# A four-layer decoder trunk on one core: part of the convolution's taps moved from TensorE to DVE, and three reorderings

## The chip, the cores and the metric

The kernel runs on one core of a Trainium2 chip, as one launch. A core has TensorE (PE), VectorE (DVE), ScalarE (ACT), GpSimd (POOL) and SyncE (SP), each with its own queue of instructions that runs strictly in the order in which the kernel writes it, and each waiting for the others only through semaphores. The metric is the device time of a launch in microseconds; lower is better. Times given are medians of several executions, and one more execution is recorded by the hardware profiler.

## The reference

The program is one inference step for 512 prompt tokens and 64 sample tokens (8 sequences of 8) with a width of 1024, in float32. Four layers: gMLP, Conformer convolution, latent attention (MLA), gMLP. Each layer has a mixer and a SwiGLU FFN of width 2816, both with adaLN conditioning, a residual and a LayerNorm. The convolution module is what most of the change touches:

```python
def conv_module(h, ctx, w_pw1, b_pw1, w_dw, b_dw, ln_g, ln_b, w_pw2, b_pw2):
    a = h @ w_pw1 + b_pw1
    a = a[..., :D_MODEL] * jax.nn.sigmoid(a[..., D_MODEL:])
    full = jnp.concatenate([ctx, a], 1)
    y = lax.conv_general_dilated(full, w_dw[:, None, :], window_strides=(1,), padding='VALID',
                                 dimension_numbers=('NWC', 'WIO', 'NWC'),
                                 feature_group_count=D_MODEL) + b_dw      # 31 taps per channel
    y = jax.nn.silu(layer_norm(y, ln_g, ln_b))
    return y @ w_pw2 + b_pw2, full[:, -(CONV_WIDTH - 1):]
```

In the attention layer `d = h @ w_down` is cut into 384 query latents, 256 key latents and 64 rotary columns; the first two are RMS-normalised, the last rotated. The FFN is `(silu(h @ wg) * (h @ wu)) @ wd`.

## The kernel before

Activations are kept transposed, channels on partitions in 8 tiles of 128 and the 576 tokens along the free dimension, in two halves of 288. Weights come from HBM in units of 1024 columns through five slots (SP's queue); GpSimd splits each unit into an upper part (`w_hi`, L1001) and the rest (`w_lo`, L1004), and every product is made of three passes in a reduced-precision float32 form: upper by upper, rest of the activation by upper, upper by rest of the weight (L1153 records all matmuls). PSUM has 8 banks: 0 to 3 take the products in turn (`acc_ready`, `acc_free`), 4 to 7 the auxiliary results (`aux_ready`, `aux_free`).

**Convolution (layer 1).** The loop runs over the 8 channel tiles m. TensorE makes the four half products of tile m + 2 (none for m = 0, 6 and 7; each half of gate and value), then tile m's taps: `x4` holds the gated rows of 32 channels at four shifts on 128 partitions, `diag` the tap weights spread on diagonals (GpSimd, L1013), and 8 groups g of 4 matmuls each, one for each 32 channels, add four taps at a time in one PSUM bank. Then come two transposes for the new state rows (L1776, L1778). ScalarE makes the sigmoid of a gate half (L2339) and issues the four DMAs that fill `x4` for tile m + 2 (`spread`, L2442). DVE's `taps(m)` gates tile m + 2's halves (L3292), completes its sample rows (L3334, L3336), adds tile m - 1 and its square to the running sums `s_sum` and `s_sq` (L3364), reduces the products that GpSimd made for the sample tokens (L3343), adds the bias on the way out of PSUM (L3367) and copies the state rows (L3350). ScalarE squares the tile (L2460). Tile 7's taps are made in two halves, with LayerNorm statistics between them.

**FFN.** From the fourth column tile on, gate and up of a tile are made by seven products in place of eight (`paired`, in the order 1, 6, 5, 7, 2, 3, 4), from sums of weights and of activations: t1, t3 and t4 are sums of activation tiles, s4 a sum of weights (`form_last`, L3049). Product 2 takes the bank of product 1, which is freed by DVE's L3084; that one reads ScalarE's copy of product 1 (L2317), which stands on ScalarE's queue behind the upper part of s4 (L2314). t4's sum is finished by L3155, its parts by L2309 (ScalarE) and L3159 (DVE). On ScalarE, `apply` (L2127) makes the modulated input in two halves; between them it runs `early`, the first two gates of what follows.

**Attention (layer 2).** DVE copies the token-major down projection to `dtok`; scales the queries; scales and rotates the key latents of the first four token tiles; TensorE transposes the queries three times over (five transposes each, two auxiliary banks each), and DVE splits each into `ql_hi` and `ql_lo` (L2643, L2645). Then TensorE waits for the key latents, transposes them (L1868) into banks 0 to 3, waits until ScalarE has copied these, and makes the ten rotary query products.

## Time and profile before

| | |
|---|---|
| median of 3 executions | 3003.37 us (3003.17 to 3003.87) |
| the profiled execution | 3006.55 us, span 3004.8 us |
| TensorE busy | 2908.9 us, 97% of the span |
| DVE, ScalarE, GpSimd busy | 1643.8, 926.0, 1699.8 us |
| mean granted TensorE clock | 0.991 of full speed (2.4 GHz) |
| chain that ended last | 81% TensorE, 7% DVE, 3% ScalarE, 2% GpSimd |

The span begins with the first recorded instruction and ends with the last; the execution's own time is 1.75 us longer. The first column of a timeline row is the start in microseconds, the second the time taken; what stands in brackets is how long the engine was idle before it, and what released it.

### The profile page before, as it was taken

What the parts mean: (1) busy time and instruction counts of PE and PEld (TensorE: products, weight loads), DVE (VectorE), ACT (ScalarE), POOL (GpSimd) and SP (SyncE); (2) the same over time, 40 slices, a digit from 0 to 9 for tenths busy, and PEclk for the clock granted to TensorE, in tenths of its full rate; (3) what the DMA queues carried; (4) which work ended last, traced back from release to release, by engine and by line L of the source; (5) the groups of instructions that cost most, each with busy time, mean ns of one, the idle gap of its engine ahead of it and who ended that gap; (6) DMA issues with size and microseconds to landing.
All of it is one profiled execution on the core that took longest, in us unless ns stands there. A gap on an engine that the chain in (4) does not pass through costs nothing.

```text
span 3004.8 us, 53453 instructions
## 1 busy us (share of the span) xinstructions
PE 2908.9 (97%) x21220; PEld 2681.8 (89%) x21220; DVE 1643.8 (55%) x3121; ACT 926.0 (31%) x1813; POOL 1699.8 (57%) x1177
## 2 busy tenths in 40 slices
PE   5999999999999999999989999999999999999997
PEld 4789999999976799999976689999997999999997
DVE  3153684636563784636565548463663536856363
ACT  2220142414230352414233315241423301425141
POOL 2546546868655445857620044685764465468685
PEclk8999999999999999999999999999999999999999
DMA  6643434333344434444321334444422333222332
GB/s 229 249 112 92 124 116 162 99 113 112 100 121 134 170 116 160 151 136 148 97 64 44 95 124 136 148 146 141 140 79 85 96 91 103 67 82 85 88 96 74
DMA packets 450485, 354.84 MB, mean 118 GB/s; under 512 B 26120, under 2 KB 424832, under 8 KB 437933
## 3 DMA queue, kind: packets, MB, share of 16 engines
q1 hardware_dynamic: 435744, 324.79, 35.1%
q10 hardware_dynamic: 14493, 26.63, 3.0%
q8 instruction: 169, 2.77, 0.4%
q14 instruction: 79, 0.65, 0.1%
HBM read 337.86 MB, written 5.25 MB: 114 GB/s over the span
## 4 chain that ended last, share of the span: by engine, by line
PE 81%; DVE 7%; issue 3%; ACT 3%; POOL 2%; DVEq 1%; DMA 1%; POOLq 1%; ACTq 1%; SPq 1%
PE pb L1153 79%; POOL w_lo L1004 1%; DMA ada_first<-in_ada_w 1%; DVE part L2778 1%; ACT h_hi L2145 1%; POOLq L1003 1%; ACT hf L2145 1%; DVE pb L2797 1%; PE pb L1989 1%; DVE xa L2804 0%; DVE h_lo L2828 0%; DVE pr L3107 0%; PE pb L1266 0%; DVE part L2773 0%; ACTq L2442 0%
## 5 line engine op out<-in xcount | busy, mean ns | idle before, releaser
L1001 POOL TENSOR_SCALAR w_hi<-w_raw 128x1024 fp32r<-128x1024 f32 (+2 forms) x272 | 295.9, 1088 | 751.0 <-DMA w_raw<-in_gmlp_w_in 275.7
L1004 POOL TENSOR_TENSOR w_lo<-w_raw,w_hi 128x1024 fp32r<-128x1024 f32 (+2 forms) x272 | 653.1, 2401 | 45.0 <-issue 45.0
L1153 PE MATMUL pb<-a_hi,w_hi 128*128 128x288 f32 x2176 | 593.8, 297 | 2.1 <-DVEq L3392 1.9
L1153 PE MATMUL pb<-a_lo,w_hi 128*128 128x288 f32 x2176 | 588.4, 294 | 0.0
L1153 PE MATMUL pb<-h_hi,w_hi 128*128 128x288 f32 x2144 | 563.9, 299 | 18.0 <-DVE pr L3084 7.9
L1153 PE MATMUL pb<-h_lo,w_hi 128*128 128x288 f32 x2144 | 545.6, 296 | 0.0
L1046 POOL TENSOR_TENSOR w_lo<-w_raw,w_hi 128x512 fp32r<-128x512 f32 x288 | 382.3, 1349 | 180.0 <-DVE s_raw L3049 83.2
L1153 PEld LDWEIGHTS pb<-h_hi,w_hi 128*128 128x128 f32 x2144 | 392.8, 188 | 33.4 <-DVE pr L3084 10.9
L1153 PEld LDWEIGHTS pb<-a_hi,w_hi 128*128 128x128 f32 x2176 | 408.3, 188 | 8.8 <-POOL a_lo L1071 4.2
L1153 PEld LDWEIGHTS pb<-a_lo,w_hi 128*128 128x128 f32 x2176 | 408.6, 188 | 0.8
L1153 PEld LDWEIGHTS pb<-h_lo,w_hi 128*128 128x128 f32 x2144 | 389.5, 189 | 0.0
L1153 PE MATMUL pb<-h_hi,w_lo 128*128 128x288 f32 x2144 | 358.1, 296 | 0.0
L1153 PE MATMUL pb<-a_hi,w_lo 128*128 128x288 f32 x2176 | 352.1, 295 | 0.3
L1153 PEld LDWEIGHTS pb<-h_hi,w_lo 128*128 128x128 f32 x2144 | 310.1, 188 | 0.5
L1153 PEld LDWEIGHTS pb<-a_hi,w_lo 128*128 128x128 f32 x2176 | 309.7, 188 | 0.9 <-POOL w_lo L1004 0.9
L2763 DVE SCALAR_TENSOR_TENSOR xa<-pb,gate,xa 128x288 f32<-128x288 f32 (+1 forms) x288 | 137.7, 479 | 269.1 <-PE pb L1153 268.0
L1153 PE MATMUL pb<-t_lo,w_hi 128*128 128x288 f32 x864 | 236.8, 295 | 0.0
L1153 PE MATMUL pb<-t_hi,w_hi 128*128 128x288 f32 x864 | 236.1, 296 | 0.0
L1153 PEld LDWEIGHTS pb<-t_hi,w_hi 128*128 128x128 f32 x864 | 162.2, 188 | 0.4
L1153 PEld LDWEIGHTS pb<-t_lo,w_hi 128*128 128x128 f32 x864 | 162.4, 188 | 0.0
L1054 POOL TENSOR_TENSOR w_raw<-w_raw 128x512 f32<-128x512 f32 x72 | 93.2, 1294 | 108.9 <-DVE pb L3040 108.9
L2255 ACT ACTIVATE w_hi<-pb 128x512 fp32r<-128x512 f32 x144 | 78.3, 597 | 239.7 <-DVE pb L3043 143.3
(379 smaller groups left out, 4875.9 us busy)
## 6 DMA issues: line engine op xcount, KB each, us to landing
ada_w<-in_ada_w SPq DMA_DIRECT2D x80, 1024.0 KB, 7.7
w_raw<-in_ffn_w_gate SPq DMA_DIRECT2D x88, 512.0 KB, 3.8
w_raw<-in_ffn_w_up SPq DMA_DIRECT2D x88, 512.0 KB, 3.8
w_raw<-in_gmlp_w_in SPq DMA_DIRECT2D x64, 512.0 KB, 4.2
w_raw<-in_ffn_w_down SPq DMA_DIRECT2D x64, 512.0 KB, 4.3
w_raw<-in_gmlp_w_out SPq DMA_DIRECT2D x32, 512.0 KB, 4.7
w_raw<-in_ffn_w_down SPq DMA_DIRECT2D x32, 384.0 KB, 3.9
w_raw<-in_conv_w_pw SPq DMA_DIRECT2D x24, 512.0 KB, 3.9
```

Source lines behind the costliest of these rows:

```text
L1001: nc.gpsimd.tensor_scalar(w_hi[:, s, 0:w], w_raw[:, s, 0:w], 1.0, 1.0, ALU.mult, ALU.mult).then_inc(split_hi, 1)
L1003: pool.drain()
L1004: nc.gpsimd.tensor_tensor(w_lo[:, s, 0:w], w_raw[:, s, 0:w], w_hi[:, s, 0:w].bitcast(F32), ALU.subtract).then_inc(split_lo, 1)
L1046: nc.gpsimd.tensor_tensor(out, src, hi.bitcast(F32), ALU.subtract).then_inc(done, 1)
L1054: nc.gpsimd.tensor_tensor(w_raw[:, su, 0:HALF_UNIT], w_raw[:, sg_, 0:HALF_UNIT], w_raw[:, su, 0:HALF_UNIT], ALU.subtract)
L1153: return nc.tensor.matmul(out, lhsT, rhs, start=start, stop=stop)
L1989: last = nc.tensor.transpose(pb[:, n % BANKS, i * P:(i + 1) * P], rows, ident[:])
L2145: last = fn(dst, xa[:, m, h * HALF:h * HALF + w], ACT.Identity, scale=cs[:, t % RING_T, m, 0:1], bias=cb[:, t % RING_T, m, 0:1])
L2255: fn(w_hi[:, SLOTS - 1, e * HALF_UNIT:(e + 1) * HALF_UNIT], pb[:, sum_banks[l][e], :], ACT.Copy).then_inc(form_hi, 1)
L2763: last_ = v.scalar_tensor_tensor(out=y, in0=ps[:, 0:w], scalar=gp, in1=y, op0=ALU.mult, op1=ALU.add)
L2778: v.reduce_sum(part[:, 1, n, half_cols(h)], sq[:, m0:m1, half_cols(h)].rearrange("p m t -> p t m"), AX.X)
L2797: v.reciprocal(self.rstd, self.rstd)
```

## The change

In the convolution TensorE makes only the first 6, 5, 5, 5, 5, 6, 8 and 8 groups of taps of the eight tiles (`PE_TAPS`), and the diagonals are made for these only. DVE adds the other taps, 7 + 4 x 11 + 7 = 58 in all, in the PSUM bank, each by one scalar_tensor_tensor over 512 tokens. ScalarE completes the sample rows, adds the bias on the way out of PSUM, and copies the state rows; GpSimd adds to the running sums. In the attention layer the query split is shared by ScalarE (upper part) and DVE (rest), the query products come before the key transposes, the key latents are made between DVE's copies of the query products, and the keys go through the auxiliary banks. In the FFN `form_last` of the first pair comes before the last sum of t4, and t4's two parts come after the copy of product 1 (ScalarE) and the second sum (DVE). In `apply` an activation of one column with the function of the coming gates (Silu or Sigmoid) stands before `early`.

The diff, cut: semaphores, the wider `epsl` and most unchanged lines are left out, and 8 columns of the indent; hunks are headed by the line of before.

```diff
@@ 117 @@
 XW = SEQ + QT * (TG - 1)
+PE_TAPS = (6, 5, 5, 5, 5, 6, TG, TG)
@@ 1011 @@
         last = nc.gpsimd.tensor_tensor(
-            diag[:, m % 2, q], mask4[:].unsqueeze(1).to_broadcast([P, TG, QC]),
-            w4[:, q, m, :].unsqueeze(2).to_broadcast([P, TG, QC]), ALU.mult)
+            diag[:, m % 2, q, 0:PE_TAPS[m]], mask4[:].unsqueeze(1).to_broadcast([P, PE_TAPS[m], QC]),
+            w4[:, q, m, 0:PE_TAPS[m]].unsqueeze(2).to_broadcast([P, PE_TAPS[m], QC]), ALU.mult)
@@ 1033 @@
             diagonals(m + 1)
+        if m >= 2:
+            pool.wait_ge(ysq_ready, m - 1)
+            pool.drain()
+            nc.gpsimd.tensor_tensor(s_sum[:], s_sum[:], yc[:, m - 2, :], ALU.add)
+            nc.gpsimd.tensor_tensor(s_sq[:], s_sq[:], sqy[:, m % 2, :], ALU.add).then_inc(q_done, 1)
@@ 1764 @@
-        for g in range(TG):
+        for g in range(PE_TAPS[m]):
...
                 last = mm(out[QC * q:QC * (q + 1), 0:c1 - c0], diag[:, m % 2, q, g, :],
-                          x4[:, m % 2, q, QT * g + c0:QT * g + c1], g == 0, g == TG - 1)
+                          x4[:, m % 2, q, QT * g + c0:QT * g + c1], g == 0, g == PE_TAPS[m] - 1)
@@ 1797 @@
         pe.wait_ge(x4_full[m % 2], 16 * QT * (m // 2 + 1))
+        conv_banks[m] = (BANKS + X.n % BANKS, BANKS + (X.n + 1) % BANKS)
...
         if m < KT - 1:
-            new_rows(pb[:, aux_bank(), :], m).then_inc(aux_ready, 1)
+            new_rows(pb[:, aux_bank(), :], m).then_inc(rows_turned, 1)
@@ 1855 @@
     pe.wait_ge(ql_scaled, 1)
+    ql_at.append(X.n)
     for k in range(3):
-        transposes([(tt * P, dtok[:, tt, k * P:(k + 1) * P]) for tt in range(4)])
-        transposes([(0, dtok[:, 4, k * P:(k + 1) * P])])
-    pe.wait_ge(kv_ready, 1)
-    pe.wait_ge(acc_free, G.n + BANKS)
-    for k in range(3):
-        for tt in range(TT):
-            rows = (ckv[:, tt, k * P:(k + 1) * P] if k < 2
-                    else kr2[:, tt, :, :].rearrange("p a n -> p (a n)"))
-            out = pb[:, k, tt * P:(tt + 1) * P] if tt < 4 else pb[:, 3, k * P:(k + 1) * P]
-            last = nc.tensor.transpose(out, rows, ident[:])
-        last.then_inc(kt_ready, 1)
-    pe.wait_ge(kt_copied, 5)
+        for tts in (range(4), (4,)):
+            b = aux_bank()
+            for tt in tts:
+                last = nc.tensor.transpose(pb[:, b, tt % 4 * P:(tt % 4 + 1) * P],
+                                           dtok[:, tt, k * P:(k + 1) * P], ident[:])
+            last.then_inc(ql_turned, 1)
+            X.up()
...
                       (lambda k: ql_hi[:, k, token_tile(tt)], lambda k: ql_lo[:, k, token_tile(tt)]))
+    pe.wait_ge(kv_ready, 1)
+    pe.wait_ge(aux_free, X.n + BANKS)
+    keys_at.append(X.n)
+    banks = [BANKS + (X.n + i) % BANKS for i in range(BANKS)]
+    for k in range(3):
+        for tt in range(TT):
+            rows = (ckv[:, tt, k * P:(k + 1) * P] if k < 2
+                    else kr2[:, tt, :, :].rearrange("p a n -> p (a n)"))
+            out = pb[:, banks[k], tt * P:(tt + 1) * P] if tt < 4 else pb[:, banks[3], k * P:(k + 1) * P]
+            last = nc.tensor.transpose(out, rows, ident[:])
+        last.then_inc(kt_ready, 1)
+    X.up(BANKS)
@@ 1903 @@
             absorb(h - 1)
+        else:
+            pe.wait_ge(aux_free, X.n + BANKS)
@@ 2131 @@
             if h:
+                if t % 2:
+                    fn(epsl[:, 4:5], epsl[:, 0:1], ACT.Silu)
+                elif t // 2 % 3 == 1:
+                    fn(epsl[:, 4:5], epsl[:, 0:1], ACT.Sigmoid)
@@ 2304 @@
         first_upper(l, 5, g0)
-        act.wait_ge(t_sum, 4 * l + 4)
-        act.wait_ge(t_lo_dve, 3 * l + 3)
-        fn(t4_hi[:], t4_raw[:], ACT.Copy).then_inc(t_hi, 1)
         G.up(8)
-        residuals(t, 10, 12)
...
         fn(sg[:, 0, :], pb[:, G.n % BANKS, 0:HALF], ACT.Copy).then_inc(pair_kept, 1)
+        if m == PAIRED_FROM:
+            act.wait_ge(t_sum, 4 * l + 4)
+            act.wait_ge(t_lo_dve, 3 * l + 3)
+            fn(t4_hi[:], t4_raw[:], ACT.Copy).then_inc(t_hi, 1)
+            residuals(t, 10, 12)
@@ 2441 @@
+    def complete(m):
+        fs = full_s(full[:, m % 3, :])
+        if m > 2:
+            act.wait_ge(prod_ready, m - 2)
+        fn(fs[:, :, 0:CTX], one(stT, m).rearrange("p (b r) -> p b r", b=DEC_B), ACT.Copy)
+        fn(fs[:, :, CTX:], bt(snew[:, m % 3, :]), ACT.Copy)
+        act.drain().then_inc(full_ready, 1)
+    def output(m):
+        ys, bd = one(yc, m, slice(SEQ, TOK)), one1(par, m, C_DW)
+        act.wait_ge(taps_summed, m + 1)
+        fn(one(yc, m, slice(0, SEQ)), pb[:, conv_banks[m][0], :], ACT.Identity, bias=bd
+           ).then_inc(aux_free, 1)
+        fn(ys, ys, ACT.Identity, bias=bd)
+        act.drain().then_inc(yc_ready, 1)
+    def state_rows(m):
+        act.wait_ge(rows_turned, m + 1)
+        for dst, n, c0 in ((st_p, CTX, 0), (st_s, NS, P)):
+            last = fn(dst[:, m * P:(m + 1) * P], pb[0:n, conv_banks[m][1], c0:c0 + P], ACT.Copy)
+        last.then_inc(aux_free, 1)
@@ 2453 @@
             spread(m + 2)
-        act.wait_ge(yc_ready, m + 1)
+            complete(m + 2)
+        if m < KT - 1:
+            output(m)
+        else:
+            act.wait_ge(yc_ready, m + 1)
...
         fn(sqy[:, m % 2, cols], yc[:, m, cols], ACT.Square).then_inc(ysq_ready, 1)
+        if m < KT - 1:
+            state_rows(m)
@@ 2515 @@
     square_sums(1, KVR, QR, range(4))
+    def query_upper(k):
+        b_p, b_s = [BANKS + (ql_at[0] + 2 * k + i) % BANKS for i in range(2)]
+        act.wait_ge(ql_turned, 2 * k + 2)
+        fn(ql_hi[:, k, 0:SEQ], pb[:, b_p, :], ACT.Copy)
+        fn(ql_hi[:, k, SEQ:], pb[:, b_s, NS:P], ACT.Copy).then_inc(ql_upper, 1)
+    for k in range(2):
+        query_upper(k)
     square_sums(1, KVR, QR, range(4, TT))
-    for k in range(3):
-        act.wait_ge(kt_ready, k + 1)
-        fn(ckvT[:, k, 0:SEQ] if k < 2 else krT[:, 0:SEQ], pb[:, k, :], ACT.Copy).then_inc(kt_copied, 1)
-    fn(ckvT[:, :, SEQ:], pb[:, 3, 0:2 * P].rearrange("p (k t) -> p k t", k=2)[:, :, NS:], ACT.Copy
-       ).then_inc(kt_copied, 1)
-    fn(krT[:, SEQ:], pb[:, 3, 2 * P + NS:3 * P], ACT.Copy).then_inc(kt_copied, 1)
+    query_upper(2)
@@ 2530 @@
                   ).then_inc(kv_out, 16)
+    key_banks = [BANKS + (keys_at[0] + i) % BANKS for i in range(BANKS)]
+    for k in range(3):
+        act.wait_ge(kt_ready, k + 1)
+        fn(ckvT[:, k, 0:SEQ] if k < 2 else krT[:, 0:SEQ], pb[:, key_banks[k], :], ACT.Copy
+           ).then_inc(aux_free, 1)
+    ps = pb[:, key_banks[3], :]
+    fn(ckvT[:, :, SEQ:], ps[:, 0:2 * P].rearrange("p (k t) -> p k t", k=2)[:, :, NS:], ACT.Copy)
+    fn(krT[:, SEQ:], ps[:, 2 * P + NS:3 * P], ACT.Copy)
+    act.drain().then_inc(aux_free, 1)
@@ 3075 @@
     u23, u4, c11, c12, c22 = pr[:, 0, :], sg[:, 1, :], sg[:, 0, :], sg[:, 1, :], pr[:, 1, :]
-    form_last(l, m)
     if m != PAIRED_FROM:
+        form_last(l, m)
@@ 3085 @@
     v.tensor_tensor(u4, p5, u23, ALU.add)
+    if m == PAIRED_FROM:
+        dve.wait_ge(t_hi, 4 * l + 4)
+        v.tensor_tensor(t4_lo[:], t4_raw[:], t4_hi[:].bitcast(F32), ALU.subtract).then_inc(t_low, 1)
@@ 3151 @@
         first_product(5, g0, 1)
+        form_last(l, ms[0])
...
         first_lower(l, 5, g0, 1)
-        dve.wait_ge(t_hi, 4 * l + 4)
-        v.tensor_tensor(t4_lo[:], t4_raw[:], t4_hi[:].bitcast(F32), ALU.subtract).then_inc(t_low, 1)
@@ 3354 @@
         if m < KT - 2:
-            for h in range(2):
-                gated_in(m + 2, h, h)
+            gated_in(m + 2, 0, 0)
+            if m:
+                dve.wait_ge(full_ready, m)
+            gated_in(m + 2, 1, 1)
             dve.drain().then_inc(rows_ready, 1)
-            complete(m + 2)
-        if m:
-            dve.wait_ge(ysq_ready, m)
-            for acc, y in ((s_sum, yc[:, m - 1, :]), (s_sq, sqy[:, (m - 1) % 2, :])):
-                last_ = v.tensor_tensor(acc[:], acc[:], y, ALU.add)
-            last_.then_inc(q_done, 1)
-        sample_taps(m)
-        v.tensor_scalar(one(yc, m, slice(0, SEQ)), pb[:, aux(), :], one1(par, m, C_DW), None, ALU.add
-                        ).then_inc(aux_free, 1)
-        dve.drain().then_inc(yc_ready, 1)
-        state_rows(m, aux()).then_inc(aux_free, 1)
+        dve.wait_ge(prod_ready, m + 1)
+        v.reduce_sum(bt(one(yc, m, slice(SEQ, TOK))), prods[m % 2][:], AX.X).then_inc(prod_used, 1)
+        sums_ = pb[:, aux(), :]
+        for w in range(QT * PE_TAPS[m], CW):
+            v.scalar_tensor_tensor(out=sums_, in0=full[:, m % 3, w:w + SEQ], scalar=wdT[:, m, w:w + 1],
+                                   in1=sums_, op0=ALU.mult, op1=ALU.add)
+            dve.drain()
+        dve.drain().then_inc(taps_summed, 1)
+        X.up()
...
     m, bd = KT - 1, one1(par, KT - 1, C_DW)
+    dve.wait_ge(yc_ready, KT - 1)
@@ 3455 @@
-    def latents(n, t0, t1):
+    def scale_keys(n, t0, t1):
@@ 3464 @@
                                    scalar=ssq[:, tt, 1:2], in1=gqk[:, QR:], op0=ALU.mult, op1=ALU.mult)
+    def turn_keys(t0, t1):
@@ 3481 @@
-    def evac_latents(ks):
-        for k in ks:
-            for cols, src in ((slice(0, SEQ), slice(0, SEQ)), (slice(SEQ, TOK), slice(NS, P))):
-                split(ql_hi[:, k, cols], ql_lo[:, k, cols], pb[:, aux(), src]).then_inc(aux_free, 1)
+    def query_lower(k):
+        dve.wait_ge(ql_upper, k + 1)
+        for cols, src in ((slice(0, SEQ), slice(0, SEQ)), (slice(SEQ, TOK), slice(NS, P))):
+            v.tensor_tensor(ql_lo[:, k, cols], pb[:, aux_of(X.n), src], ql_hi[:, k, cols].bitcast(F32),
+                            ALU.subtract).then_inc(aux_free, 1)
+            X.up()
+    def query_rows(n):
+        c, tt = divmod(n, TT)
+        dve.wait_ge(acc_ready, G.n + 1)
+        v.tensor_copy(qrt[:, tt, c * 256:(c + 1) * 256], pb[:, G.n % BANKS, 0:256]).then_inc(acc_free, 1)
+        G.up()
@@ 3499 @@
                 scale_queries()
-            if tt == TT - 2:
-                latents(2, 0, 4)
-    evac_latents((0,))
-    latents(3, 4, TT)
+    for k in range(3):
+        query_lower(k)
+    dve.drain().then_inc(lat_ready, 1)
+    scale_keys(2, 0, 4)
+    for n in range(2):
+        query_rows(n)
+    turn_keys(0, 4)
+    for n in range(2, 5):
+        query_rows(n)
+    scale_keys(3, 4, TT)
+    turn_keys(4, TT)
     dve.sem_inc(kv_ready, 1)
-    evac_latents((1, 2))
-    dve.drain().then_inc(lat_ready, 1)
-    for c in range(2):
-        for tt in range(TT):
-            dve.wait_ge(acc_ready, G.n + 1)
-            v.tensor_copy(qrt[:, tt, c * 256:(c + 1) * 256], pb[:, G.n % BANKS, 0:256]
-                          ).then_inc(acc_free, 1)
-            G.up()
+    for n in range(5, 10):
+        query_rows(n)
+    X.up(BANKS)
```

## Rows read from the trace of the kernel before

**Rows 1.** The page, part 1: busy time, share of the span, instructions.

```profile
PE 2908.9 (97%) x21220; PEld 2681.8 (89%) x21220; DVE 1643.8 (55%) x3121; ACT 926.0 (31%) x1813; POOL 1699.8 (57%) x1177
```

**Rows 2.** Two tiles: length, each engine's busy time, clock, DMA share, GB/s.

```profile
893.20:913.20 20.00, 20.00 (x163) 14.81 (x162) 13.76 (x15) 1.58 (x3) 15.97 (x10) 1.00 0.45 109
933.20:953.30 20.10, 20.10 (x165) 14.91 (x164) 6.77 (x12) 1.69 (x3) 13.36 (x9) 1.00 0.43 108
```

**Rows 3.** TensorE's timeline: tile 0's taps and what follows them.

```profile
864.30 7.08 PE L1153 MATMUL pb<-x,diag 128*32 128x512 f32 x64
...
873.13 0.40 PE L1153 MATMUL pb<-h_hi,w_hi 128*128 128x288 f32 x1 [1.43 <-DVE full L3292]
```

**Rows 4.** Instructions by source line: count, ns min/median/max, first and last start.

```profile
L3043 DVE TENSOR_TENSOR pb<-pb,w_raw x72: 698/700/700, 451.6 to 2918.7; 128x512 f32<-128x512 f32 x72
...
L2763 DVE SCALAR_TENSOR_TENSOR xa<-pb,gate,xa x288: 439/472/521, 245.3 to 2988.5; 128x288 f32<-128x288 f32 x124, 128x224 f32<-128x224 f32 x20
...
L3343 DVE TENSOR_REDUCE yc<-prod x8: 2205/2210/2221, 877.3 to 989.2; 128x64 f32<-128x1984 f32 x8
...
L3364 DVE TENSOR_TENSOR s_sum<-s_sum,yc x6: 757/759/4580, 890.9 to 977.0; 128x576 f32<-128x576 f32 x6
...
L1004 POOL TENSOR_TENSOR w_lo<-w_raw,w_hi x272: 994/2400/3482, 9.5 to 2958.5; 128x1024 fp32r<-128x1024 f32 x114, 128x768 fp32r<-128x768 f32 x18, 128x384 fp32r<-128x384 f32 x4
```

**Rows 5.** ScalarE's timeline: the residuals, and one tile's four DMA issues.

```profile
863.63 8.41 ACT L2162 ACTIVATE xa<-xa,ab,ag 128x288 f32<-128x288 f32 x16 [14.71 <-issue]
...
913.47 4.33 ACTq L2442 DMA_DIRECT2D x<-full  x4
```

**Rows 6.** Tile 7's taps in TensorE's timeline; x4's DMAs from 973 to 985.

```profile
984.39 0.94 PE L1153 MATMUL pb<-x,diag 128*32 128x288 f32 x12 [0.72 <-issue]
...
x<-full ACTq DMA_DIRECT2D x4, 270.0 KB, 7.9
```

**Rows 7.** The first pairs in FFN 0 and 1: timelines, and one stretch.

```profile
465.80 0.40 PE L1153 MATMUL pb<-h_hi,w_hi 128*128 128x288 f32 x1 [0.67 <-DVE pr L3084]
...
477.70 0.40 PE L1153 MATMUL pb<-h_hi,w_hi 128*128 128x288 f32 x1 [0.52 <-DVE pr L3084]
...
1125.15 2.51 DVE L3155 TENSOR_TENSOR t_raw<-t_raw,h_lo 128x1152 f32<-128x1152 f32 x1 [0.20 <-issue]
...
1130.38 0.69 DVE L3049 TENSOR_TENSOR s_raw<-w_raw,pb 128x512 f32<-128x512 f32 x1
...
1132.64 0.40 PE L1153 MATMUL pb<-h_hi,w_hi 128*128 128x288 f32 x1 [1.82 <-DVE pr L3084]
...
1132.60:1136.40 3.80, 3.75 (x17) 3.76 (x18) 3.27 (x7) 2.17 (x4) 2.33 (x2) 0.56 0.02 4
```

**Rows 8.** Timelines: a table load in layer 3, TensorE's waits behind the gates.

```profile
834.72 0.54 PE L1153 MATMUL pb<-h_hi,w_hi 128*128 128x288 f32 x2 [0.70 <-DVEq L2837]
...
2594.98 1.28 ACT L2203 ACT_TABLE_LOAD   x1 [5.33 <-PE pb L1153]
...
2599.17 0.54 PE L1153 MATMUL pb<-h_hi,w_hi 128*128 128x288 f32 x2 [2.69 <-DVEq L2837]
```

**Rows 9.** The attention layer's transposes: DVE, TensorE, and two stretches.

```profile
1545.12 0.69 DVE L2643 CAST ql_hi<-pb 128x512 fp32r<-128x512 f32 x1
1545.89 0.69 DVE L2645 TENSOR_TENSOR ql_lo<-pb,ql_hi 128x512 fp32r<-128x512 f32 x1
...
1546.64 1.33 PE L1266 MATMUL pb<-ident,dtok 128*128 128x128 f32 x5 [5.38 <-DVE ql_lo L2645]
1549.40 0.90 PE L1868 MATMUL pb<-ident,ckv 128*128 128x128 f32 x3 [1.44 <-DVEq L3482]
...
1553.83 0.39 PE L1153 MATMUL pb<-w_hi,ql_hi 128*128 128x256 f32 x1 [0.97 <-ACT krT L2524]
...
1546.60:1554.00 7.40, 4.95 (x21) 4.16 (x22) 5.35 (x19) 2.08 (x5) 1.55 (x3) 0.58 0.91 264
1554.00:1565.00 11.00, 11.00 (x93) 11.00 (x93) 3.89 (x10) 0.00 (x0) 4.48 (x6) 1.00 0.29 83
```

More of the change, by code:

```diff
@@ L206, in trunk @@
         mtmp = sb("mtmp", [P, KT, NC])
-        epsl = at("epsl", [P, 2], F32, top[0] - 32)
+        epsl = at("epsl", [P, 8], F32, top[0] - 32)
         ada_row_at = region(size([P, TOK]))
@@ L433, in trunk @@
         taps_done = sem("taps_done")
+        taps_summed = sem("taps_summed")
+        rows_turned = sem("rows_turned")
         last_tile = sem("last_tile")
@@ L447, in trunk @@
         kt_ready = sem("kt_ready")
-        kt_copied = sem("kt_copied")
+        ql_turned = sem("ql_turned")
+        ql_upper = sem("ql_upper")
         ql_scaled = sem("ql_scaled")
@@ L757, in trunk @@
         turn_at = []
+        conv_banks = {}
+        ql_at, keys_at = [], []
         stat_banks = {}
```

## The prediction, made before the changed kernel was built or run

> **What bounds the kernel now.** I read the first part of the page, then the stretches between two convolution tiles, then TensorE's idle times in order of time, and behind each the instruction that ended it. TensorE is busy for 2908.9 of 3004.8 us [rows 1]: a gain is either matmul work taken off it, or one of its waits, or a stretch that it ran at the low clock after a wait. In the convolution it is busy all of the time, 20.05 us a tile (mean of 20.00 and 20.10), while DVE is busy for 6.8 to 13.8 us and GpSimd for 13.4 to 16.0 [rows 2]. The sum is made against the profiled execution's 3006.55 us (1.75 us around the span); the median shown, 3003.37, is 3.2 us less.
>
> **Convolution, matmuls removed.** A tile of 8 tap groups takes 7.07 us [rows 3], with the last matmul's own tail in it, so a group is 0.87 us. Tiles 1 to 4 lose 3 groups each, 12 x 0.87 = 10.4 us; tiles 0 and 5 lose 2 each, 1.7 us. The saving counts only where nothing else ends TensorE's next wait.
> - Tile 0: behind it TensorE already waits 1.43 us for DVE's gated rows [rows 3]. These wait for ScalarE's gate, which starts when 16 residual instructions end (863.63 + 8.41 = 872.04) [rows 5]; none of this depends on the taps. Its 1.7 us become wait: 3.1 us idle in one piece. 1.82 us of idle in layer 1 were followed by a stretch of 3.8 us at a mean granted clock of 0.56 [rows 7], part of it at 1.2 GHz in place of 2.4, which costs 0.44 x 3.8 = 1.6 us; the 1.43 us here were not. I count 0 gained and 1.6 lost; bounds 0 and -1.7.
> - Tiles 1 to 4: 10.4, if DVE, ScalarE and GpSimd keep up with 20.05 - 2.6 = 17.4 us (below).
> - Tile 5: 1.7, but tile 7's taps, two tiles on, waited 0.72 us for something the trace names no releaser for, and its x4 copies take 7.9 us to land behind 4 MB of adaLN weights [rows 6]. I take 1.0, between 0 and 1.7.
>
> **Does DVE keep up?** Added: 58 scalar_tensor_tensor of 128x512, read from SBUF and PSUM, written to PSUM, each with a drain. This form isn't in the trace. From below: tensor_tensor with the same two homes and size, 0.70 us; from above: scalar_tensor_tensor of 128x288, at most 0.52, by columns 0.93 [rows 4]. Start to start over a drain two dependent instructions are 0.77 us apart, 0.08 more than one lasts [rows 9]. I take 0.78 + 0.08 = 0.86 (bounds 0.78 and 1.01): 11 taps 9.5 us, 58 taps 50. Three gated rows (at most 1.5) and the sample reduction (2.2) [rows 4] make 13.2 us a tile. DVE becomes the bound at (17.4 - 3.7)/11 = 1.25 us a tap, and the tile is slower than before at 1.49. The Trainium skill (VectorE: DVE Perf Modes, The DRAIN you can't avoid) states a flush of about the duration less 266 ns behind every DVE instruction; an estimate by that page is 0.78 + 0.51 = 1.29 us a tap, and DVE would be the bound by 0.04 x 11 = 0.4 us a tile; the 0.77 us pair speaks against it.
>
> More is at stake in blocking. GpSimd works for most of the tile, and a DVE addition of two SBUF tiles that takes 0.76 us took 4.58 once; the additions with one input in PSUM never exceeded 0.70 in 72 cases [rows 4], GpSimd or not. The taps are of the second kind. What leaves DVE (two running sums, copies, bias) was partly of the first.
>
> ScalarE per tile: two gates, 4.3 us of DMA issues [rows 5], now also two copies, bias of 512 and 64 columns, the square, two state-row copies: some 4 us by the 0.5 to 0.7 us that such instructions take. In order: taps summed at 9.5 after the matmuls' end, bias, square and rows until 11.7, and only then the next tile's first gate, queued behind the wait for the sums, until 12.3, DVE's gated row 12.8. TensorE asks for that bank at 17.4: slack 4.6. The last gate's pair is ready at 13, DVE ends its reduction at 16.8, before the next tile's sums: slack 0.6, and lateness there is not passed on at once, as the output bank is needed only two tiles later.
>
> GpSimd per tile: 13.36 busy [rows 2] (its diagonals get shorter, which I leave out), plus two sums of 576 columns (w_lo's 1024 take 2.40 [rows 4], by columns 1.35, I take 1.45): 16.3 of 17.4. In the tail the sums and the products wait for ScalarE's copies, so the five weight splits behind them start about 5 us later and run into DVE's a_lo subtractions, which are of the blocked kind: 0.3 lost.
>
> **Tables.** The gate's ACT_TABLE_LOAD stood behind TensorE's product (5.33 us of ScalarE idle, 1.28 of load, then the gates) [rows 8]. Now a dummy draws it into that idle time; the half-block that follows on ScalarE and DVE starts 1.28 earlier. TensorE waits there for 2.69 us in layer 3 and 0.70 before the convolution [rows 8]; in layers 0 to 2 it has adaLN matmuls to run and no such wait. Gain 1.28 + 0.70 = 2.0. The Trainium skill (ScalarE: Activation LUTs, What ACT_TABLE_LOAD costs) puts a switch at 2.66 us with its drain; by that the gain would be 2.66 + 0.70 = 3.4, but the rows show the gates start 1.29 us behind the load's start.
>
> **FFN.** PSUM bank 0 is freed by DVE's L3084, which waits for ScalarE's copy, which stands behind the copy of s_raw, which waits for L3049, which stands behind t4_lo and the t4 sum, L3155. In layer 1: L3155 at 1125.15 for 2.51, L3049 at 1130.38, TensorE released at 1132.64 after 1.82 us [rows 7]. With form_last ahead of L3155, s_raw is made at some 1125.8 and copied while L3155 runs; L3084 then follows L3155 (1127.66) and one subtraction of 0.5, near 1128.3, while TensorE is through its fourth product at 1130.8 (1132.64 - 1.82). The wait goes (four layers: 0.67, 1.82, 1.86, 1.81; two shown). So does the low clock behind the last three, 1.6 each. What is late next: t4_lo (1.36) now lies between L3087 and the sums of the second pair, and GpSimd's s_lo can block it; layer 0 shows the second pair's wait, 0.52 [rows 7], which layers 1 to 3 hid by the low clock. I take 0.8 in each. Layer 0: 0.67 - 0.3 = 0.4. Layers 1 to 3: 3 x (1.83 + 1.6 - 0.8) = 7.9. Sum 8.3, bounds 2 (the second wait brings the low clock back) and 10.
>
> **Attention.** TensorE waits 5.38 + 1.44 + 0.97 = 7.8 us around the two sets of transposes, and the clock is 0.58 over 7.4 us with 4.95 busy: 0.42 x 4.95 = 2.1 lost [rows 9]. The first wait is for the first query split, which DVE begins at 1545.12, behind the key latents in its queue. Afterwards DVE and ScalarE share the split at once: ScalarE's copies of 512 and 64 columns 0.8 us, DVE's two subtractions 0.9. The third pair of transposes waits about 0.9, the products about 1.95 for the last split: 2.85, and I expect one low-clock stretch behind it, 1.6. The key latents then run under the ten query products, which fill the 11.0 us from 1554 on [rows 9]: some 9 us of DVE work by its instructions of 0.2 to 0.5, ready about 2 us before TensorE asks. Gain 9.9 - 4.45 = 5.4, bounds 3 and 7. SP's loads behind d_ready (value weights, masks, head units) move ahead with it, GpSimd's splits too; four output DMAs on ScalarE's queue stand ahead of the key copies, 2.7 us, covered by the first head's two products.
>
> **Sum.** 10.4 + 0 - 1.6 + 1.0 - 0.3 + 2.0 + 8.3 + 5.4 = 25.2 us. 3006.55 - 25.2 = 2981.4 as profiled, 2978.2 as timed. A change below 0.2%, 6 us, can't be told from none.
>
> **Rivals.**
> - GpSimd or the ring DVE, ScalarE, DVE sets the tile. It decides once GpSimd's 16.3 or DVE's 16.8 us exceed 17.4, say by port conflicts. At the full 20.05 the 10.4 are lost: 2988.6. For: the slack is 1.1 and 0.6. Against: both lag by up to a tile without harm. Chance 0.10.
> - On the other side: the taps are blocked by GpSimd after all, as s_sum once was [rows 4]. The trace has no scalar_tensor_tensor with in0 in SBUF and in1 in PSUM. At 2.4 us a tap a tile takes 3.7 + 26.4 = 30 us: +10 in four tiles, +40 - (25.2 - 11.4) = +26: 3029. It decides at 1.49 us a tap for the tiles, and at about 1.8 for the whole. The Trainium skill (SBUF — State Buffer, Who interferes with whom) says that an instruction with at most one SBUF input does not contend; the 72 rows agree. Chance 0.04.
> - The low clock does not come back (tile 0, attention): 3.2 more, 2975; with small second waits in the FFN, 2973. For: 1.43 us of idle did not bring it [rows 3]. Against: 1.82 did [rows 7]. Chance 0.2.
> - The waits move rather than go: attention 3, FFN 2 to 4: 2985. Chance 0.13.
> - The forecast, 2974 to 2983: chance 0.53.
>
> From 2971 to 2988 some 8 in 10 are held: below lies a part of the clock's case, above it the blocked taps and most of the first rival. Faster 0.94 (all but the blocked taps and 2 in 100 in which several gains fail), same 0.02, slower 0.04.
>
> **What would show it.** Right: tile windows of 17.4 us with TensorE full from tile 1 to 4; 58 instructions of 0.7 to 0.9 us, longest near the median; no L3084 wait in the first pair, one below 1 us in the second; two waits near 0.9 and 2 us before the queries and none before the keys; a wait of 3 us behind tile 0. Wrong: taps with a long tail of durations; TensorE waiting for w_lo or the gated rows in tiles 2 to 5; a low clock in tiles 1 to 4; the keys awaited.

## The result and the profile after

The changed kernel takes 2978.2 us (median of 4 executions, 2974.5 to 2981.6) against 3003.6 (4 executions, 3003.2 to 3004.7): a ratio of 0.9915 with a 95% interval of 0.9897 to 0.9932. The forecast was 2978.2, range 2971 to 2988. The profiled execution is the shortest of the four, 2974.5 us with a span of 2972.4. It gained 32.4 us of span, seven more than the 25.4 between the medians; where the seven come from is told below.

The first part of the page, which answers to [rows 1]:

```profile
span 2972.4 us, 53309 instructions
PE 2887.9 (97%) x21092; PEld 2669.5 (90%) x21092; DVE 1643.3 (55%) x3121; ACT 941.8 (32%) x1864; POOL 1713.7 (58%) x1189
```

TensorE's busy time fell by 21.0 us and the rest of the span by 11.4. Two tiles, by windows (columns: window, its length, busy time of PE, PEld, DVE, ACT, POOL, granted clock, DMA share, GB/s), and the new instruction by its line:

```profile
889.40:906.80 17.40, 17.40 (x142) 14.03 (x138) 11.62 (x16) 3.59 (x9) 16.91 (x12) 1.00 0.51 124
924.20:941.60 17.40, 17.40 (x142) 14.07 (x138) 11.62 (x16) 3.63 (x9) 16.39 (x12) 1.00 0.51 128
```

```profile
L3440 DVE SCALAR_TENSOR_TENSOR pb<-full,wdT,pb x58: 745/755/758, 874.6 to 966.6; 128x512 f32<-128x512 f32 x58
```

Against [rows 2] a tile is 2.65 us shorter and TensorE is as full as before. All 58 taps take 745 to 758 ns; nine in a row take 7.39 us, so 0.83 from one to the next. GpSimd is busy for 16.4 and 16.9 of the 17.4 us, where 16.3 had been forecast.

TensorE's idle times by the timeline (start of the instruction that ended the wait, its duration, then in brackets the wait and its releaser), those that answer to [rows 3], [rows 6], [rows 7], [rows 8] and [rows 9]:

```profile
477.53 0.40 PE L1164 MATMUL pb<-h_hi,w_hi 128*128 128x288 f32 x1 [1.06 <-DVE pr L3156]
...
871.88 0.40 PE L1164 MATMUL pb<-h_hi,w_hi 128*128 128x288 f32 x1 [2.84 <-DVE full L3366]
973.76 1.61 PE L1164 MATMUL pb<-x,diag 128*32 128x288 f32 x21 [1.83 <-issue]
...
1128.21 0.40 PE L1164 MATMUL pb<-h_hi,w_hi 128*128 128x288 f32 x1 [0.78 <-DVE pr L3156]
...
1523.44 0.77 PE L1875 MATMUL pb<-ident,dtok 128*128 128x128 f32 x5 [0.99 <-DVE ql_lo L3565]
1525.91 0.58 PE L1164 MATMUL pb<-w_hi,ql_hi 128*128 128x256 f32 x1 [1.71 <-DVEq L3591]
1534.50 0.39 PE L1164 MATMUL pb<-w_hi,ql_hi 128*128 128x256 f32 x1 [0.60 <-DVE qrt L3573]
1538.83 0.39 PE L1164 MATMUL pb<-w_hi,ql_hi 128*128 128x256 f32 x1 [0.84 <-DVE qrt L3573]
...
2570.39 0.53 PE L1164 MATMUL pb<-h_hi,w_hi 128*128 128x288 f32 x2 [2.18 <-DVEq L2909]
```

L3156 is the L3084 of before. Behind the 2.84 us comes a stretch at half clock, in windows:

```profile
873.40:876.80 3.40, 3.40 (x17) 3.40 (x16) 3.24 (x4) 0.02 (x1) 3.40 (x2) 0.50 0.85 125
877.00:889.40 12.40, 12.40 (x103) 10.14 (x105) 5.74 (x9) 3.37 (x9) 12.07 (x10) 1.00 0.44 131
```

TensorE is full in it at 0.50 (1.2 GHz), so it costs 1.7 us.

**Where the time went, step by step.** Each kernel was traced a second time (`before_again` and `repeat` below). The span is cut at the same TensorE instructions in all four traces; a gain is the stretch's length before less that after. The first pair is the first trace of each kernel, the second pair the second.

| stretch | predicted | first pair | second pair |
|---|---|---|---|
| FFN, layer 0 | 0.4 | 0.5 | 0.4 |
| to the first taps (gate table) | 0.7 | 0.7 | 1.0 |
| tile 0 | -1.6 | -1.2 | -2.9 |
| tiles 1 to 4 | 10.4 | 10.3 | 10.3 |
| tile 5 until tile 7's taps | 1.0 | 0.6 | 0.5 |
| convolution's tail | -0.3 | 0.1 | 0.1 |
| FFN, layers 1, 2, 3 | 7.9 | 3.7, 3.2, 2.6 | 3.8, 3.1, 1.8 |
| attention, until the first head's end | 5.4 | 4.3 | 4.1 |
| layer 3's wait (gate table) | 1.3 | 0.5 | 0.5 |
| **steps of the prediction** | **25.2** | **25.2** | **22.7** |
| not edited: start of layer 1 | 0 | 3.8 | 0.6 |
| not edited: all the rest | 0 | 3.4 | -3.2 |
| **span** | | **32.4** (3004.8 to 2972.4) | **20.1** (2999.2 to 2979.1) |

The steps account for what changed in their own stretches. The seven microseconds by which the first pair exceeds them are in stretches where nothing was edited. The last row also holds the products right behind layer 3's wait: the half clock there was in the kernel before in the first pair and in the changed kernel in the second, 1.0 us for and 1.0 against the change.

### The profile page after: what moved, and what is told of

It reads as the page before. It is cut to its first block, busy times and chain, and to the rows that moved or that the text cites. A ratio compares the mean times of both kernels' runs of the same rounds, so it can differ in the third digit from the quotient of the medians.

```text
span 2972.4 us, 53309 instructions
## 1 busy us (share of the span) xinstructions
PE 2887.9 (97%) x21092; PEld 2669.5 (90%) x21092; DVE 1643.3 (55%) x3121; ACT 941.8 (32%) x1864; POOL 1713.7 (58%) x1189
## 4 chain that ended last, share of the span: by engine, by line
PE 80%; DVE 8%; issue 3%; ACT 2%; POOL 2%; DVEq 1%; POOLq 1%; DMA 1%; ACTq 1%; SPq 1%
PE pb L1164 79%; POOL w_lo L1010 1%; DMA ada_first<-in_ada_w 1%; DVE part L2850 1%; POOLq L1009 1%; ACT h_hi L2171 1%; ACT hf L2171 1%; DVE pb L2869 1%; DVE xa L2876 1%; PE pb L2011 0%; DVE pr L3182 0%; DVE h_lo L2900 0%; DVE part L2845 0%; POOL w_lo L1057 0%; DVEq L2875 0%
```

## The experiments

**The changed kernel once more** (no edit).

> The changed kernel once more, nothing edited. Its first profiled execution gained 32.4 us of span (3004.8 to 2972.4) where the steps sum to 25.2, and its four times spread over 7 us (2974.5 to 2981.6), against 1.6 us for the kernel before. Theory A, phase: at the start of layer 1 DVE's L2788 and L2793 (all operands in SBUF) run beside or ahead of GpSimd's weight split by luck; in the kernel before they took 1.11 and 2.35 us, TensorE waited 2.62 us, and a 3.4 us stretch at half clock followed; here 0.23 and 0.93, no wait, full clock. In this second trace one or more of the three stretches that were at the low clock before (1050, 1730, 2600 us) comes back, each worth 1.3 to 3.8 us, and the span is 2974 to 2981. Theory B: these gains belong to the change; then the same two low-clock stretches (at the convolution's first tile and in the attention) and no other are seen, and the span is within 1 us of 2972.4. Ratio to before in both: 0.9905 to 0.993.

2979.5 us (5 executions, 2976.2 to 2983.8), ratio 0.9918 (0.9904 to 0.9931); profiled 2981.2, span 2979.1. Between 60 and 2950 us TensorE's records show 17.1 us at half clock, where the first trace had 6.8: at 64, 872 (twice as long), 1531 and 2576 us. Half of the difference is 5.1 us of time; 2.8 us more are waits (39.7 against 36.9 us of TensorE's idle time from 380 us on). The two overlap, since a wait costs nothing more at half clock; together they cover the 6.7 us between the two spans, and the clock has the larger part. Theory A holds in that stretches come back; but of the three that I had named only the one at 2600 did (at 2576), and DVE was ahead of GpSimd again.

**The kernel before once more** (no edit).

> The kernel before once more, nothing edited: a second trace of it. Its profiled execution took 3006.6 us, with 27.3 us of half clock between 60 and 2950 us and a wait of 2.62 us at 1050 us behind DVE's L2716 and L2721 at 1.11 and 2.35 us, which began 0.03 us after GpSimd's weight split. Theory: whether these two are blocked is decided by which engine starts first, and in most traces (seven of nine so far) DVE does; then they take 0.23 and 0.23 to 0.93 here, the 2.62 us wait is gone and the span is 2998 to 3003. Rival: in this kernel GpSimd always comes first, and the change moved that; then 1.11, 2.35 and 2.6 us again. The ratio to the kernel before is 1 within 0.001, which shows what the measurement can tell.

Median 3004.9 (10 executions, 3001.0 to 3007.8), ratio 1.0005 (0.9996 to 1.0014), so a difference of 0.1%, 3 us, can just be told. The trace has span 2999.2 and 13.7 us at half clock, against 27.3 in the first. At the start of layer 1, DVE and GpSimd by the timeline, first in the first trace of before, then in this one:

```profile
1033.30 1.11 DVE L2716 SCALAR_TENSOR_TENSOR cs<-mtmp,par 128x72 f32<-128x72 f32 x1
1034.33 0.22 DVE L2718 SCALAR_TENSOR_TENSOR mtmp<-mtmp,par 128x72 f32<-128x72 f32 x1
1034.62 2.35 DVE L2721 TENSOR_TENSOR cb<-cb,mtmp 128x72 f32<-128x72 f32 x1
...
1033.27 1.06 POOL L1001 TENSOR_SCALAR w_hi<-w_raw 128x1024 fp32r<-128x1024 f32 x1 [34.71 <-DMA w_raw<-in_conv_w_pw]
```

```profile
1033.69 0.23 DVE L2716 SCALAR_TENSOR_TENSOR cs<-mtmp,par 128x72 f32<-128x72 f32 x1
1033.84 1.08 DVE L2718 SCALAR_TENSOR_TENSOR mtmp<-mtmp,par 128x72 f32<-128x72 f32 x1
1034.99 0.23 DVE L2721 TENSOR_TENSOR cb<-cb,mtmp 128x72 f32<-128x72 f32 x1
...
1033.70 1.15 POOL L1001 TENSOR_SCALAR w_hi<-w_raw 128x1024 fp32r<-128x1024 f32 x1 [34.76 <-DMA w_raw<-in_conv_w_pw]
```

GpSimd starts 0.03 us ahead of L2716 in the one and 0.01 behind it in the other. From the start of L2716 to the end of L2721 DVE needs 3.67 us or 1.53; in the second trace L2718 is the one that is slow. The 2.1 us go down DVE's queue to the statistics, for which TensorE waits 2.62 us, or 0.23. With the half clock behind the longer wait that is the 3.8 us of the table: not the change's.

**The coefficients' rows in PSUM** (the edit, cut; L2788 and L2793 are the L2716 and L2721 of before).

```
-  add(mtmp[:], 0)                               # SBUF
+  mt = pb[:, bk, :].rearrange("p (b n) -> p b n", b=16)[:, 0:KT, 16:16 + NC]
+  add(mt, 0)                                    # a free part of the bank it reads
...
-  v.scalar_tensor_tensor(out=cs[:, tr], in0=mtmp[:], ...)
+  v.scalar_tensor_tensor(out=cs[:, tr], in0=mt, ...)
```

> The changed kernel with mtmp, the scale and shift rows from which DVE makes the adaLN coefficients, in a free part of the PSUM bank that they come from and not in SBUF: three instructions for each of seven sets have one SBUF input where they had two. Theory: DVE instructions with two SBUF inputs are the ones that GpSimd blocks. Then the first and the last of the three at the start of layer 1 take 0.22 to 0.3 us whatever GpSimd does beside them (0.23 and 0.93 in the changed kernel, 1.11 and 2.35 in the kernel before and in u23_apart), TensorE has no wait for the statistics at 1040 us in any run, and the times scatter less upward: 0.5 to 2 us faster in the median. Rival: GpSimd blocks them all the same, by the output in SBUF; then 0.9 to 2.4 us are seen again, and the time is the same within 1 us.

```profile
1026.28 0.23 DVE L2788 SCALAR_TENSOR_TENSOR cs<-pb,par 128x72 f32<-128x72 f32 x1
1026.73 0.23 DVE L2793 TENSOR_TENSOR cb<-cb,pb 128x72 f32<-128x72 f32 x1
...
1026.05 1.06 POOL L1007 TENSOR_SCALAR w_hi<-w_raw 128x1024 fp32r<-128x1024 f32 x1 [31.55 <-DMA w_raw<-in_conv_w_pw]
```

Here GpSimd started 0.23 us ahead of L2788, and nothing is blocked. In the seven traces of changed kernels in which L2793 ran under GpSimd's split with both inputs in SBUF, but L2788 had started first, it took 0.91 to 0.94. The time did not follow: 2979.6 us, ratio 0.9923 (0.9910 to 0.9937), the same as `repeat`, where 0.5 to 2 us had been expected. The event was rare in the changed kernels (one of ten traces with mtmp in SBUF, `u23_apart`), so there was little to win in the median.

**The taps' sum in SBUF** (the edit, cut: ScalarE's bias reads `yc` too).

```
-  v.scalar_tensor_tensor(out=sums_, in0=full[...], ..., in1=sums_)   # sums_ in PSUM
+  v.scalar_tensor_tensor(out=yc[:, m, 0:SEQ], in0=full[...], ..., in1=sums_)
+  sums_ = yc[:, m, 0:SEQ]
```

> DVE's taps keep their count and size, but their running sum is in SBUF: the first tap of a tile reads TensorE's bank and writes yc, the others (52 of 58) read full and yc and write yc, and ScalarE adds the bias there. In the changed kernel's traces all 58 taps took 746 to 758 ns with GpSimd busy for nearly all of the tile. The prediction's step: an addition with one input in PSUM isn't blocked by GpSimd, one with two inputs in SBUF is (0.76 us took 4.58 once). Then these 52 have a long tail or a median well above 0.76, the tiles 1 to 4 go from 17.4 to 22 to 30 us, TensorE waits there for the gated rows, and the kernel is 15 to 60 us slower. Rival: the home of the inputs doesn't matter, these additions just were short; then the taps stay at 0.75 to 0.8 us and the time within 2 us of the changed kernel. In between: only those taps that begin under an instruction of GpSimd wait for it, once each; at 10 or so such waits of 1 to 2.4 us a tile DVE needs 11 x 0.83 + 3.7 + 10 to 20.

```profile
L3440 DVE SCALAR_TENSOR_TENSOR yc<-full,wdT,yc x52: 750/791/4555, 877.4 to 995.7; 128x512 f32<-128x512 f32 x52
L3440 DVE SCALAR_TENSOR_TENSOR yc<-full,wdT,pb x6: 736/739/749, 876.6 to 985.0; 128x512 f32<-128x512 f32 x6
```

The 52 taps with two SBUF inputs take 79.2 us in all, 1.52 on average and up to 4.56; the six that read PSUM keep to 0.75. TensorE waits 2.3, 7.9 and 3.8 us for the gated rows of the tiles behind them, 4.2 more for ScalarE's bias ahead of tile 7's taps, and the time is 3002.7 us, ratio 0.9993 (0.9983 to 1.0002): the whole gain of the change is gone. GpSimd suffers too: its w_hi splits of 1.05 us had a median of 1.49. This is the rival "blocked by GpSimd", at a mean of 1.52 us a tap, and it shows that the input's home decided it: the six write SBUF just as the 52 do, and five of them ran beside a busy GpSimd. The Trainium skill (SBUF — State Buffer, Who interferes with whom) says that a DVE instruction with two SBUF inputs contends with a GpSimd instruction that reads SBUF, and that one with at most one SBUF input, outside the 2-port perf modes, does not; these rows agree.

**All taps on TensorE.**

```
-PE_TAPS = (6, 5, 5, 5, 5, 6, TG, TG)
+PE_TAPS = (TG,) * 8
```

> All 8 tap groups of every tile on TensorE, DVE adds no tap; ScalarE's bias, squares and copies and GpSimd's running sums stay as changed. By the prediction's sum the tiles 1 to 4 cost 10.4 more, tile 5 between 0.6 and 1.7, and tile 0 gives back the 1.6 of the low clock behind a longer wait: 9 to 11 us slower than the changed kernel, some 2988, with tiles of 20.0 us. If instead the shift of work to ScalarE and GpSimd were what gained in the tiles, the time would be within 3 us of the changed kernel. If the taps on DVE cost something elsewhere (late residual adds, blocked splits), the loss is below 8.

2988.8 us, ratio 0.9949 (0.9935 to 0.9963), 9.3 more than `repeat`, as expected. The removed matmuls are the gain of the convolution, and the move of the other work gains nothing by itself. Tile 0 is followed by a wait of 1.37 us and no half clock, as before the change.

**Tile 0 alone back on TensorE.**

```
-PE_TAPS = (6, 5, 5, 5, 5, 6, TG, TG)
+PE_TAPS = (TG, 5, 5, 5, 5, 6, TG, TG)
```

> Only tile 0 goes back to 8 groups on TensorE (its 7 taps leave DVE). Theory: tile 0 saved nothing, since the gated row came when it came, and the 2.84 us of idle behind it brought a 3.4 us stretch at half clock. With 8 groups the idle is 1.1 to 1.4 us, the clock stays full, tile 1's taps start some 1.5 us earlier relative to the wait's end, and the kernel is 1.0 to 1.8 us faster than the changed one. Rival: the low clock comes whatever the idle's length, then the time is the same within 0.5 us; or the two groups really were on the path, then it is 1.7 us slower.

2981.6 us, ratio 0.9925 (0.9912 to 0.9939), against 2979.5 for `repeat`: the 1.0 to 1.8 us expected did not come. Locally the theory held: 0.56 us of wait for the gated row, full clock, and from the last wait ahead of the convolution (817 us) to tile 1's taps it takes 67.9 us against 69.2 and 70.7 in the two traces of the changed kernel. But then two stretches of half clock stood at 974 and 1011 us, behind waits of 2.58 and 1.87 us. In the two traces of the changed kernel these waits are 1.83 and 1.95, 1.87 and 1.88 us, at the full clock. In this trace what tile 0 won was lost at them; that the edit brings the half clock there is not shown, since `coefs_psum` and `u23_apart`, with tile 0 as changed, have the second one too.

**Four groups on TensorE in tiles 1 to 4.**

```
-PE_TAPS = (6, 5, 5, 5, 5, 6, TG, TG)
+PE_TAPS = (6, 4, 4, 4, 4, 6, TG, TG)
```

> Tiles 1 to 4 keep 4 tap groups on TensorE instead of 5, DVE adds 15 taps in each instead of 11. In the changed kernel's trace nine taps take 7.39 us, 0.83 from one to the next, and DVE is busy for 11.6 of a tile of 17.4 us. Theory: a tile is then 17.4 - 0.87 = 16.53 us, DVE needs 15 x 0.83 + 3.7 = 16.15 and GpSimd some 16.3, so TensorE still sets it: 4 x 0.87 = 3.5 us faster than the changed kernel. Rival: the ring of sums, ScalarE's bias and gate, and DVE's gated row is what TensorE waits for; then the tile stays near 17.4 with TensorE idle in it, and the time is within 1 us. Rival: GpSimd at its limit slows the tiles, with waits for the weights' low parts, 0 to 2 us slower.

2981.3 us, ratio 0.9930 (0.9916 to 0.9944): not the 3.5 us faster that was expected. The rival of the ring holds. DVE and ScalarE in tiles 2 to 3:

```profile
923.88 0.52 DVE L3366 SCALAR_TENSOR_TENSOR full<-pb,par,sg 128x288 f32<-128x288 f32 x1 [2.90 <-ACT sg L2366]
...
927.21 12.38 DVE L3440 SCALAR_TENSOR_TENSOR pb<-full,wdT,pb 128x512 f32<-128x512 f32 x15
942.50 0.52 DVE L3366 SCALAR_TENSOR_TENSOR full<-pb,par,sg 128x288 f32<-128x288 f32 x1 [2.90 <-ACT sg L2366]
...
939.70 0.69 ACT L2484 ACTIVATE yc<-pb,par 128x512 f32<-128x512 f32 x1 [9.67 <-DVEq L3443]
941.88 0.87 ACT L2366 ACTIVATE sg<-pb,par 128x288 f32<-128x288 f32 x2
```

One turn is 942.50 - 923.88 = 18.6 us: 3.3 for gated rows and reduction, 12.4 for the taps, and 2.9 in which DVE stands idle while ScalarE adds the bias, squares, copies and only then makes the gate. TensorE could do a tile in 16.5 and waits, 1.02 and 1.74 us. The same idle time is in the changed kernel, with 11 taps:

```profile
920.34 0.52 DVE L3366 SCALAR_TENSOR_TENSOR full<-pb,par,sg 128x288 f32<-128x288 f32 x1 [2.91 <-ACT sg L2366]
```

There DVE waits 1.20 and 0.77 us more in a turn, for TensorE by way of the second gate and for the sums, so that TensorE sets the tile.

**The FFN's order put back** (last sums behind L3155, t4's split on ScalarE ahead of the first pair; the other edits stay).

```
-                    form_last(l, ms[0])
...
-                if m == PAIRED_FROM:
-                    dve.wait_ge(t_hi, 4 * l + 4)
-                    v.tensor_tensor(t4_lo[:], ...)
```

> Only the FFN's order is put back (last sums behind the product's sum, the fourth operand's split ahead of the first pair); the rest is as changed. Theory by the steps: layer 0 loses 0.4, layers 1 to 3 lose 1.8 of wait and 1.6 of low clock each and get 0.77 back: 3 x 2.64 + 0.4 = 8.3 us slower than the changed kernel, with waits for L3156 of 0.7 in layer 0 and 1.8 in each of the others and a 3.4 us stretch at half clock behind each of these three. Rival: the low clock depends on the phase of each run and not on the 1.8 us wait; then fewer than three such stretches are seen and the loss is 3.5 to 7 us.

2989.5 us, ratio 0.9950 (0.9936 to 0.9963), 9.9 more than `repeat`. By the traces' stretches it is 7.1: 0.9, 1.8, 2.6 and 1.8 for layers 0 to 3. The waits of 1.84, 1.82 and 1.84 us are back, but half clock stands behind the one in layer 2 only; where it is missing, the second pair's wait shows (0.53 in layers 1 and 3). The rival about the clock (fewer than three such stretches) was right; the 7.1 by the stretches is just above its 3.5 to 7, and the timed 9.9 is above both forecasts.

**The gate's table not drawn ahead** (the two dummy activations left out).

> Only the two dummy activations that draw the gate's table ahead are left out. By the prediction's step the kernel is 2.0 us slower than the changed one: 1.28 in layer 3, where TensorE waits for the second half's statistics (2.18 us in the changed kernel, 2.69 in the one before), and 0.70 at the convolution's entry, whose wait comes back. The traces gave 0.62 at the entry and 0.54 in layer 3, 1.2 together. Rival: TensorE's wait in layer 3 hangs on DVE, not on ScalarE's table; then it stays near 2.2 and only the convolution's 0.6 is lost.

2980.9 us, ratio 0.9930 (0.9915 to 0.9944): 3.6 us slower than `repeat` by the ratios, whose intervals overlap. The trace gives the size, 1.2 us where the prediction had 2.0: the wait at the convolution's entry is back at 0.69 us, and layer 3's is 2.69 where all others with the dummies have 2.17 to 2.31.

**The attention's order put back** (its edits in the diff above, reversed).

> Only the attention's order is put back (keys' transposes ahead of the queries' products, DVE alone splits the queries); the rest is as changed. By the prediction the kernel is 5.4 us slower than the changed one; its trace gave 4.3 between the last product before the transposes and the first head. The waits of 5.4, 1.4 and 1.0 us come back, and a stretch of 6.8 us at half clock. Rival: the low clock is luck here too (the changed kernel once more had 3.4 us of it in the attention, two other variants 6.8), then the loss is 2.5 to 3.5.

2983.9 us, ratio 0.9935 (0.9921 to 0.9949), 5.1 us slower than `repeat` by the ratios, whose intervals overlap a little. The waits are back at 5.39, 1.14 and 0.97 us, with 13.7 us of half clock. From the last products before the transposes to the first head's end it takes 84.5 us, against 78.9 in the changed kernel, some 5.5 more. The kernel before needs 1.2 to 1.4 less than this for the same stretch, with 6.8 us of half clock: that much of the loss is the clock's, and the rest agrees with the 4.3 and 4.1 of the table.

**A buffer of its own for the second pair's sum** (the edit, cut). In the changed kernel DVE idles for GpSimd before L3156:

```profile
1127.70 0.46 DVE L3156 TENSOR_TENSOR pr<-pb,sg 128x288 f32<-128x288 f32 x1 [3.04 <-POOL a_lo L1082]
...
1126.04 1.56 POOL L1082 TENSOR_TENSOR a_lo<-pr,a_hi 128x288 fp32r<-128x288 f32 x2
```

It waits only because the sum goes into the half of pr that GpSimd still reads.

```
+  spare = at("spare", [P, HALF], F32, a_at + HB // 2 + (KT - 1) * TOK * 4)
...
+  second = m == PAIRED_FROM + 1
+  if second: u23 = spare[:]
...
+  if second: dve.wait_ge(a_ready, 8 + a_before(l) + 2 * m)   # here, ahead of c22
```

> The changed kernel with one buffer more: in the FFN's second pair DVE writes the sum of L3156 into the idle last tile of a_lo and not over the gated values that GpSimd still reads (L1082), and waits for GpSimd only ahead of the write that follows later. Theory: the 0.77 to 1.06 us that TensorE waits for L3156 in each of the four layers are this wait, so they go: 3.4 us faster than the changed kernel, no wait for L3156 in any layer, and none for a later instruction of this pair. Rival: the wait moves to DVE's next additions (bank of the fourth product), still 0.5 to 1 us a layer, and nothing is gained. Rival: DVE's sum comes only after the copy of the first product by ScalarE, and half of it is gained.

2971.5 us, ratio 0.9893 (0.9878 to 0.9909), the lowest median of all, though its interval overlaps that of `repeat` a little. No wait for this instruction is left in any layer, and by the stretches of the four FFNs the gain is 0.9 to 1.1 each, 4.0 in all, against 3.4 expected. The rest of the 8 us between the medians stays unexplained: the trace is of the slowest of the four executions (2976.0), and the other three have none. This trace even caught the blocked coefficients:

```profile
1023.85 1.11 DVE L2789 SCALAR_TENSOR_TENSOR cs<-mtmp,par 128x72 f32<-128x72 f32 x1
1025.17 2.35 DVE L2794 TENSOR_TENSOR cb<-cb,mtmp 128x72 f32<-128x72 f32 x1
...
1023.83 1.05 POOL L1008 TENSOR_SCALAR w_hi<-w_raw 128x1024 fp32r<-128x1024 f32 x1 [31.76 <-DMA w_raw<-in_conv_w_pw]
...
1041.15 0.75 PE L1165 MATMUL pb<-part,ones 128*128 128x288 f32 x2 [2.59 <-DVEq L2852]
```

**Three edits together** (`u23_apart`, `coefs_psum`, and DVE's third query copy moved between the halves of the keys' rotation).

> The two edits together (the pair's sum in a buffer of its own, the coefficients' rows in PSUM), and in the attention DVE copies the third query product between the two halves of the keys' rotation. Expected against the changed kernel: 4.2 us from the first (four waits for L3156, as the trace of u23_apart gave them), 0.5 to 2 from the second, 0.3 to 0.8 from the third (of the waits of 0.6 and 0.84 us for the query copies one goes, but the keys are then ready about 0.8 us after TensorE asks for them): 5 to 7 us faster than the changed kernel, ratio to the kernel before 0.989 to 0.990. If the three took from one another (a wait that moves), it is 3 to 4.

2975.0 us, ratio 0.9908 (0.9893 to 0.9923), its span 2971.1: 4.5 us below `repeat` by the medians and 3.0 by the ratios, less than the 5 to 7 expected. The first edit's waits are gone again. Of the third the expected trade is seen: one query wait of 0.49 in place of 0.60 and 0.84, and a new wait of 0.64 for the keys. Its interval overlaps that of `u23_apart`; the two edits added have no gain that these runs show.

## Why the prediction was right, point by point

- **Tiles 1 to 4, 10.4:** 10.3 in both pairs. DVE's 0.86 us a tap was 0.83, and its work in a tile 12.4 (3.3 for rows and reduction, 9.1 for 11 taps) against 13.2. The estimate from the Trainium skill's flush (VectorE: DVE Perf Modes, The DRAIN you can't avoid), 1.29 us, is refuted for this case: the 0.77 us pair [rows 9] was the right row. "Taps with one input in PSUM are not blocked" is shown from both sides, by 745 to 758 ns in PSUM and by 750 to 4555 in SBUF.
- **DVE's bound was mis-sized,** though the forecast did not hang on it. I put it at (17.4 - 3.7)/11 = 1.25 us a tap, as if DVE worked through. `four_groups` shows that 2.9 us of every turn are idle, since the gated row waits for the sums by way of ScalarE: (17.4 - 3.3 - 2.9)/11 = 1.02. At five groups the turn is 15.3 us, 2.1 below the tile; at four it is 18.6 against 16.5. The 15.3 is reckoned from these parts, the 18.6 measured. I had called ScalarE's slack 4.6 and DVE's 0.6 and treated them as two; it is one ring. GpSimd's slack was smaller than said as well: 0.5 to 1.0 us a tile for 1.1.
- **Tile 0, nothing gained and 1.6 lost:** wait 2.84 and 3.34, clock at half, -1.2 and -2.9. The wait and the half clock came as said, but undoing it did not help (`tile0_8`).
- **Tile 5 and tail:** 0.6 for 1.0; the later splits of GpSimd cost nothing that shows.
- **Tables, 2.0:** 0.7 to 1.0 at the entry for 0.7, 0.5 in place of 1.28 in layer 3; this term was sized too high, and the larger 3.4 that stood beside it still more. The load's 1.28 us do come off the start of the gates, but then both gates and DVE's products wait for TensorE's last banks (0.60 to 0.73 us), which finish in that very stretch; the next bound was close behind.
- **FFN, 8.3:** 9.9 and 9.2. The second waits were as taken, 0.76 to 0.80, and the L3084 waits of the first pair are gone. What I had not counted is that the waits of 0.81 and 0.41 us for the same line in later pairs (1359 and 2128 us) went as well. The term for the clock was too sure: of nine waits of 1.81 to 1.86 us (first trace of before, `before_again`, `ffn_undone`), six had half clock behind them. In the second pair one of the three in the kernel before was missing (layer 3: 1.8 for 2.6), which hides part of what I had not counted.
- **Attention, 5.4:** 4.3 and 4.1. The two waits ahead of the products were 0.99 and 1.71, forecast 0.9 and 1.95, and one stretch of 3.4 us at half clock came. Missed: two waits of 0.60 and 0.84 us for the query copies. I had placed the key latents "under the ten query products" by their sum of work; but the copies queue behind the rotation in DVE's order, and TensorE has only four banks to run ahead. The keys themselves are not awaited, as said.
- **The number itself** came out to 0.0 us, which is luck: the time of one execution scatters by 7 us, and in the two traces of the changed kernel the larger part of this is half clock that follows a wait in one and not in the other. The steps gave 25.2 and 22.7 us in the two pairs, and the timed difference was 25.4, then 23.6 (`repeat`). In the sum FFN gave 0.9 to 1.6 us more than its term, and attention and tables gave 1.9 and 1.8 less. The mechanism is shown: the parts, undone one by one, lose 9.3 (timed), 7.1, 1.2 and 5.5 us (by the stretches).
